# Picking and returning the experts' tokens by TensorE in a mixture-of-experts layer, and v by token in the dilated attention

## The reference, cut to what matters

```python
def expert_block(args):                      # 32 experts, two for each token
    tok_b, e = args
    xb = xpad[tok_b]                         # 64 slots: rows of the normalised tokens
    h = jax.nn.silu(xb @ w_gate[e]) * (xb @ w_up[e])     # 1024 -> 2 x 512
    return h @ w_down[e]                     # 512 -> 1024
out = out.reshape(rows, d) * buf_wt[:, None]
y = jnp.zeros((t + 1, d)).at[buf_tok].add(out)[:t]       # weighted, added back by token
...
q, k, v, z = jnp.split(h @ w_in, [G * E, 2 * G * E, 2 * G * E + E], axis=-1)   # dilated_mixer
```

## Time and profile before

| | us |
|---|---|
| median of 3 runs | 1627.55 (1623.54 to 1627.7) |
| the profiled execution | 1623.5 |
| its span, first to last instruction | 1621.7 |
| PE busy | 1405.4 (87% of the span) |
| DVE busy | 658.9 (41%) |
| ACT busy | 482.8 (30%) |
| POOL busy | 84.6 (5%) |

### The profile page before, as it was taken

One profiled execution on the slowest core, in us unless ns is written; L12 is line 12 of the kernel. 1 busy time (PEld: TensorE's weight loads), 2 busy tenths in 40 slices (PEclk: granted clock), 3 DMA queues, 4 the chain that ended last, 5 costly groups with the idle time before them and its releaser, 6 DMA issues.

```text
span 1621.7 us, 17185 instructions
## 1 busy us (share of the span) xinstructions
PE 1405.4 (87%) x6530; PEld 946.7 (58%) x6530; DVE 658.9 (41%) x1144; ACT 482.8 (30%) x717; POOL 84.6 (5%) x139
## 2 busy tenths in 40 slices
PE   6999996997787779878739999989999999999976
PEld 5787774332222323322227888767788878878765
DVE  4567746010000000000065656545555654565545
ACT  6462431110000000100153222334444534544432
POOL 2010001110000000100021010000000000000000
PEclk9999996999889999988959999989999999999988
DMA  8737338999999999999774553221212122121001
GB/s 356 306 130 271 145 113 322 348 386 393 399 406 400 385 385 404 373 395 395 318 287 144 207 195 130 104 80 52 104 52 104 53 78 79 61 96 52 1 1 65
DMA packets 41004, 347.71 MB, mean 214 GB/s; under 512 B 6080, under 2 KB 6208, under 8 KB 22592
## 3 DMA queue, kind: packets, MB, share of 16 engines
q1 hardware_dynamic: 29632, 304.69, 48.3%
q0 software_dynamic: 10304, 38.84, 7.0%
q10 hardware_dynamic: 960, 2.70, 0.4%
HBM read 321.56 MB, written 24.64 MB: 213 GB/s over the span
## 4 chain that ended last, share of the span: by engine, by line
PE 48%; DVE 3%; ACT 2%; issue 2%; DMA 1%; DVEq 0%; POOL 0%; SPq 0%; ACTq 0%; POOLq 0%
PE ps L259 46%; PE ps L649 1%; ACT ar L798 1%; DVE b_NL L1242 0%; DVE ar L1234 0%; DMA ar<-y_scratch,rt 0%; PE ps L708 0%; DVE hres L1676 0%; ACT ar L811 0%; PE ps L265 0%; DVE hres L1669 0%; ACT b_NH L807 0%; DMA y_scratch<-ar 0%; DVE ar L1856 0%; ACT ar L1012 0%
## 5 line engine op out<-in xcount | busy, mean ns | idle before, releaser
L259 PE MATMUL ps<-ring,ar 128*64 128x512 f32 x720 | 266.8, 640 | 61.5 <-issue 49.2
L259 PE MATMUL ps<-ar 128*128 128x128 f32 (+6 forms) x1022 | 290.5, 439 | 12.8 <-DVE ar L1587 4.6
L259 PE MATMUL ps<-b_NH,b_WH 128*128 128x512 f32 x768 | 203.7, 401 | 9.3 <-ACT b_NH L807 4.2
L1617 DVE TENSOR_TENSOR ar<-ar,ps 128x256 f32<-128x256 f32 x34 | 14.3, 422 | 482.1 <-ACT ar L939 482.1
L259 PEld LDWEIGHTS ps<-ring,ar 128*64 128x64 f32 x720 | 78.3, 146 | 224.0 <-issue 206.2
L259 PE MATMUL ps<-b_NH,b_WL 128*128 128x512 f32 x768 | 197.4, 393 | 0.0
L259 PE MATMUL ps<-b_NL,b_WH 128*128 128x512 f32 x768 | 190.4, 391 | 0.0
L1175 DVE TENSOR_TENSOR b_WL<-ring,b_WH 128x1024 fp32r<-128x1024 f32 x112 | 136.7, 1221 | 99.5 <-ACT b_WH L750 99.5
L259 PEld LDWEIGHTS ps<-b_NH,b_WH 128*128 128x128 f32 x768 | 142.1, 190 | 40.7 <-ACT b_NH L807 8.9
L259 PEld LDWEIGHTS ps<-b_NH,b_WL 128*128 128x128 f32 x768 | 145.9, 190 | 30.6
L259 PEld LDWEIGHTS ps<-b_NL,b_WH 128*128 128x128 f32 x768 | 144.9, 189 | 30.2
(11 more groups left out here) (260 smaller groups left out, 1550.7 us busy)
## 6 DMA issues: line engine op xcount, KB each, us to landing
ring<-in_wts_dram SPq DMA_DIRECT2D x79, 2048.0 KB, 17.4
spare<-in_wts_dram SPq DMA_DIRECT2D x31, 2048.0 KB, 37.4
ar<-in_wts_dram SPq DMA_DIRECT2D x22, 2048.0 KB, 39.7
ring<-in_wmod_dram SPq DMA_DIRECT2D x24, 512.0 KB, 5.0
ar<-in_wmod_dram POOLq DMA_DIRECT2D x24, 512.0 KB, 4.2
y_scratch<-gate POOLq DMA_DIRECT2D x11, 1024.0 KB, 21.1
y_scratch<-ar SPq DMA_DIRECT2D x68, 128.0 KB, 31.7
hres<-in_x_dram SPq DMA_DIRECT2D x4, 512.0 KB, 5.9
```

The lines of the kernel that those rows point to most:

```text
L259: return pe.matmul(o, l, m, start=start, stop=stop, skip_group_check=True)
L1617: return dve.tensor_tensor(hh[s], sg[s], ps[:, b, 256:512], ALU.mult)
```

## The change

The rows of an expert are picked by a product with a matrix of ones and noughts, and its results are brought to their tokens by a product with a matrix of weights and noughts and added to `hres` by DVE from PSUM. The gathers, stores, both DRAM copies, the noughts and the table are gone. The experts' buffers are single (two for `ysb`); the panels have eight slots. Each expert's result is returned during the next expert, a second block's within its own turn.

```diff
+            def rows_in(b):
+                for p in range(4):
+                    mm(ps[0:64, b, :], OH[:, p, :], xs[:, p, 0:512], p == 0, p == 3)
+                    t = mm(ps[64:128, b, :], OH[:, p, :], xs[:, p, 512:1024], p == 0, p == 3)
+            def turn_x(b):
+                for j in range(4):
+                    t = pe.transpose(ps[:, b, j * 128:(j + 1) * 128], xg[:, j * 128:(j + 1) * 128], ident[:, :])
-            def turn_x(s, b):
-                for k in range(8):
-                    t = pe.transpose(ps[:, b, k * 64:(k + 1) * 64], xg[s][0:64, k * 128:(k + 1) * 128],
-                                     ident[0:64, 0:64])
+            def rows_out(ys, p, b, sem):
+                for hf in range(2):
+                    r = slice(64 * hf, 64 * hf + 64)
+                    mm(ps[:, b + hf, :], OT[r, p * 128:(p + 1) * 128], ys[r, :], True, True).then_inc(S[sem], 1)
+            def main_out(n, p):
+                if p == 0:
+                    pe.wait_ge(S["m_ot"], n + 1)
+                    pe.wait_ge(S["m_y"], n + 1)
+                if 8 * n + 2 * p >= 2:
+                    pe.wait_ge(S["m_ad"], 8 * n + 2 * p)
+                rows_out(ysb[n % 2], p, 6, "m_sc")
```

PE's order in one expert after the change (waits on panels and buffers left out), and for a second block:

```diff
             for n in range(NE):
+                up(xT, 0, (panel(i), panel(i + 1))).then_inc(S["m_up"], 1)
+                if n:
+                    main_out(n - 1, 0)
                 pe.wait_ge(S["m_hh"], n + 1)
+                turn_h(4).then_inc(S["m_d1"], 1)
+                    rows_in(2).then_inc(S["m_gx"], 1)
+                if n:
+                    main_out(n - 1, 1)
+                down(5, panel(i + 2)).then_inc(S["m_d2"], 1)
+                    turn_x(3).then_inc(S["m_tx"], 1)
+                if n:
+                    main_out(n - 1, 2)
+                    main_out(n - 1, 3)
                 with pe.If(second(n)):
+                    rows_in(2).then_inc(S["o_gx"], 1)
+                    turn_x(3).then_inc(S["o_tx"], 1)
+                    up(xT2, 1, (panel(i), panel(i + 1))).then_inc(S["o_up"], 1)
+                    turn_h(4).then_inc(S["o_d1"], 1)
+                    down(5, panel(i + 2)).then_inc(S["o_d2"], 1)
+                    for p in range(4):
+                        if p:
+                            pe.wait_ge(S["o_ad"], 8 * n + 2 * p)
+                        rows_out(ysb[1 - n % 2], p, 6, "o_sc")
+                    pe.wait_ge(S["o_ad"], 8 * n + 8)
```

```diff
+            def pick_in(n, sem, e, ne):
+                dve.tensor_scalar(rel, sl_f, float(-CAP * n), None, ALU.add).then_inc(S[e], 1)
+                dve.tensor_tensor(eq, bc(mid(i_n[:, 0:CAP]), 128, 8, CAP), bc(last(rel), 128, 8, CAP),
+                                  ALU.is_equal).then_inc(S[e], 1)
+                dve.tensor_tensor(OH, eq[:, 0:4, :], eq[:, 4:8, :], ALU.add).then_inc(S[sem], 1)
+            def pick_out(n, sem, e, ne):
+                for c, o in enumerate((OT, ot1)):
+                    dve.scalar_tensor_tensor(out=o, in0=slrow[c], scalar=jn[:, n:n + 1], in1=wrow[c], op0=ALU.is_equal,
+                                             op1=ALU.mult).then_inc(S[e], 1)
+                dve.tensor_tensor(OT, OT, ot1, ALU.add).then_inc(S[sem], 1)
+            def add_out(p, hf):
+                h = hres[:, p, hf * 512:hf * 512 + 512]
+                return dve.tensor_tensor(h, ps[:, 6 + hf, :], h, ALU.add)
```

In the dilated attention v is projected by token in two panels after head 0's first four tiles (`token_panel(P_V, ...)`, 96 products each, as many as eight v tiles had), and ACT evicts it straight to `vall`. The other 56 tiles follow through three banks in place of two, and the last two are the z tiles of heads 6 and 7, behind which attention steps 0 and 1 of head 7 lie:

```diff
-                    if j == 3:
-                        pe.wait_ge(S["vc"], h + 1)
-                        for q in range(4):
-                            t = pe.transpose(ps[:, 5, q * 128:(q + 1) * 128], sw[(7 * h + 6) % 2][:, q * 128:(q + 1) * 128],
-                                             ident[:, :])
-            for step in range(6):
+            for step in range(2, 6):
                 attention(7, step)
```

More of the change, by code:

```diff
@@ L713, in tensor_program, with first, behind @@
-            for step in range(6):
+                h, r = TILES[g]
+                if r == 6:
+                    pe.wait_ge(S["z"], h + 1)
+                else:
+                    pe.wait_ge(S["ra"], 6 * h + r + 1)
+            def first(j):
+                if j == 3:
+                    proj_free(0)
+            def behind(g):
+                if g >= 7:
+                    proj_free(g - 3)
+            b4 = tuple(PROJ[g % 3] for g in range(4))
+            lead_panel(P_DIL, op_b, N_DL, b4)
@@ new lines, in tensor_program @@
+            run(feature_tiles(P_DIL, op_b, b4, (2, 3), first))
+            token_panel(P_V, op_b, (2, 3, 4, 6))
+            proj_free(3)
+            pe.wait_ge(S["vk"], 2)
+            token_panel(P_V + 1, op_b, (7, 0, 2, 3))
+            proj_free(1)
+            proj_free(2)
+            for q in range(1, 14):
+                i = P_V + 1 + q
+                b4 = tuple(PROJ[(4 * q + j) % 3] for j in range(4))
+                for j in feature_tiles(i, op_b, b4, range(4), lambda j, q=q: behind(4 * q + j)):
+                    h, step = step_behind(4 * q + j)
+                    if h >= 0 and step < 6:
+                        attention(h, step)
@@ L935, in scalar_program, with copy_x @@
             act.activation(ex, t1_, ACT.Exp).then_inc(S["rt_act"], 1)
[L938 to L945 removed]
+            def copy_x():
+                return act.activation(xg, ps[:, 2, :], ACT.Copy)
@@ new lines, in silu_gate, with copy_h, copy_y, copy_rows @@
+            def silu_gate(b):
+                return act.activation(sg, ps[:, b, 0:256], ACT.Silu)
+            def copy_h():
+                return act.activation(hT.rearrange("p a b -> p (a b)"), ps[:, 4, 0:256], ACT.Copy)
+            def copy_y(s):
+                return act.activation(ysb[s], ps[:, 5, :], ACT.Copy)
+            def copy_rows(dst, u):
+                act.wait_ge(S["rw"], u + 1)
+                for c in range(2):
+                    act.activation(dst[c], ps[:, 6 + c, :], ACT.Copy).then_inc(S["rwc"], 1)
@@ L1151, in scalar_program @@
-            for step in range(6):
+            for g in range(4):
+                if g < 2:
+                    hi(P_DIL, g + 2)
+                elif g == 3:
+                    hi(P_V, 0)
+                rope(g)
+            for c in range(2):
+                for n in range(4):
+                    next_hi(P_V + c, n)
+                for t in range(4):
+                    evict(P_V + c, t, vall[:, t, c * 512:(c + 1) * 512], ACT.Copy, "vk",
+                          ((2, 3, 4, 6), (7, 0, 2, 3))[c][t])
@@ L1152, in scalar_program @@
+            for g in range(4, 56):
+                next_hi(tile_panel(g), g % 4)
+                if TILES[g][1] < 6:
+                    rope(g)
+                else:
+                    silu_z(g)
+                h, step = step_behind(g)
+                if h >= 0 and step < 6:
+                    attention(h, step)
+            for step in range(2, 6):
                 attention(7, step)
-            act.wait_ge(S["wdone"], done(cno(P_DIL + 15, 3)))
+            act.wait_ge(S["wdone"], done(cno(P_DO - 1, 3)))
```

718 lines of the change are left out of this document (327 added, 391 removed).

## The result

| | before | after |
|---|---|---|
| median, us | 1626.01 (4 runs, 1623.54 to 1627.70) | 1875.89 (4 runs, 1870.31 to 1880.77) |
| span of the profiled execution | 1621.7 | 1876.5 |
| PE busy | 1405.4 (87%) | 1670.4 (89%) |
| DVE busy | 658.9 (41%) | 936.3 (50%) |

What follows compares the result with a forecast made beforehand. The prediction took DMA bytes to bound the experts and TensorE the dilated attention, with TensorE bounding the experts after. It summed 1623.5 + 192 (experts) - 1 (start) - 3.5 (tail) - 15 (v) = 1796 us, range 1735 to 1860.

Steps and rivals of the forecast that it cites:

- pure column time: Experts: TensorE's products alone, before any wait, take 17.9 us per expert, above the 16.2 us at which DMA would bind.
- The turn: Experts 1 to 30: products, returns, waits and branch in order on TensorE sum to 20.8 us per expert.
- about 0.4 shows: Each expert: of PE's branch on second(n), about 0.4 us is not covered by queued products, estimated from ACT's dozen branches.
- Rival 2: Experts: idle bursts halve PE's clock, costing 1.7 us per turn, +54 us in all, 1850 us; chance 0.07.
- The second blocks: Two experts' extra blocks become a chain of products, waits and returns on PE: 32 us each, 64 us together.
- Twelve branches (1.9 us on DVE): Tail after the last expert: returns, these branches and pick_out bring the first addition to about +10 us; tail -3.5 us.
- The start: From slot numbers to the first up: picking replaces gathering, first up at about 276 us, -1 us, at best -5.
- v by token: Dilated attention: ACT-eviction waits and four transposes per head go, and head 7's steps move earlier: -15 us.
- The changes between kinds of product: Experts on TensorE: 0.1 us at each switch of product kind, about nine per expert; uncertainty 0 to 0.2 us each.
- Serial halves (1): Returns: products on the two row halves take turns, +2.6 us per expert, +81 in all, 1881 us; chance 0.08.
- DMA stays the bound (3): Experts: PE has room, so the stage shrinks to its panels' 479 us, -51, total 1553 us; chance 0.03.
- A hidden wait (4): Experts: PE's queue hides the fourth return's wait, branches cost nothing: 18.8 us per expert, 1728 us; chance 0.07.

Runs made afterwards that it cites:

- experiment 3: The changed kernel with each expert's fourth return in two other PSUM banks, so it no longer waits for the third's additions: 1784.22 us, ratio 1.099.
- experiment 4: The changed kernel without any branch among the experts, second and overflow blocks left out, the fourth return's wait kept: 1739.03 us in one execution.
- experiment 1: The twelve untaken overflow-block branches removed on all engines: from the changed kernel 1844.39 us, ratio 1.136; from the kernel before 1621.64 us, ratio 0.998.
- experiment 8: The kernel before with only the changed dilated attention: 1611.47 us, ratio 0.991; with the twelve overflow branches also inside one: 1609.19 us.
- experiment 5: The kernel of experiment 3 with each product of the returns issued twice into the same bank: 1891.30 us in one execution.

## Why the prediction was right or wrong

**The bound and the sign: right.** TensorE became the bound and DMA fell to 0.63. The forecast's 17.9 us of pure column time, above the panels' 16.3 (16.2 in the forecast), decided it; experiment 3, whose plain turns have no wait left, puts 19.2 us on TensorE.

**The turn, 20.8 us forecast, 21.6 measured.** The single term most in error is the branch, "about 0.4 shows": it costs 0.76 (experiment 4). The wait was 1.37, not 1.6, and the products with their changes together some 0.65 more than the 18.8: the fourth return takes 1.13 in place of 0.9, and no other part is off by more than 0.15. Over 30 turns that is +24 us. Taking ACT's dozen branches as the price of PE's was the weak choice: ACT's are 0.15 us apart, while PE's branch and what stands around it hold its queue for 1.8 us, of which the fourth return covers 1.1.

**The clock: wrong to leave out as small.** Rival 2 had 0.07 and 1.7 us per lost turn. The price was right (1.65), the number of turns was neither all nor none but 7 of 28: +12 us. The forecast treated the clock as a case of its own, and so its sum held nothing for it.

**The second blocks, 32 us forecast, 38 measured:** +12. The chain was right; the forecast ran it at 2.4 GHz, although its rival 2 says that PE stands idle for half of their returns.

**The tail, the largest error.** "Twelve branches (1.9 us on DVE)" is the step that failed: -3.5 forecast, +27.1 measured. The 1.9 us are ACT's, from the earlier trace rows (DVE's own twelve take 2.1 in that trace), and the walk of PE itself, 28.6 us in the kernel after, was left out of the sum. The kernel before has it in its trace (15.9 us), inside the 25.25 us that its timeline puts down to ACT before the first transposes:

```profile
832.68 1.94 PE L265 MATMUL ps<-ident,ar 128*128 128x128 f32 x8 [25.25 <-ACT ar L1016]
```

This is a step that was moved past a queue: the last returns now stand behind branches that nobody waited for before. Experiment 1 shows it: without the branches the tail is 25.5 us shorter. The +-5 for start and tail were drawn without this row, and without this error the time would have lain inside the range, near its upper end.

**The start, -1 forecast:** from slot numbers to the first silu it is 22.4 to 22.7 us in the five profiles of the old form and 16.3 to 16.6 in the eight of the new, 6 us less. Half of this lies before the first up (12.5 us before, 9.3 after), which is what the forecast's -1 to -5 was about, and half in that up itself (10.3 and 7.1 us): rows_in now runs ahead of it, and the granted clock is back at 2.4 GHz when it starts. In this execution slot numbers came 6.2 us late, as TensorE ran at half clock from 153 to 167 us in code that the change does not touch; three of the five profiles of the old form have such a stretch there too.

**v by token, -15 forecast:** -14.8, and -13.6 to -14.9 alone (experiment 8).

**The changes between kinds of product.** The sum had 0.1 us at each, from one row; the two forms of return (1.06 us alone, 0.86 and 0.2 in experiment 5) give the same. The Trainium skill (TensorEngine Tiling, Key Properties) says that a change of tiling mode drains TensorE; the trace agrees in that a return's second pair and the product behind it each start some 0.1 us behind the steady pace. A turn has eight changes (the forecast says about nine), some 0.8 us of 21.6.

**The rivals.** Serial halves (1): refuted by the records' starts, 0.007 us apart, and by experiment 5. DMA stays the bound (3): refuted by DMA at 0.63 and by experiment 3. A hidden wait (4): experiment 3 builds that kernel, and it takes 19.2 us per turn where 18.8 were forecast. Of the 80 us missed in all, 24 are the turn, 12 the clock, 12 the second blocks, 30 the tail; what is left is under the spread of the runs.

## What to carry to other kernels

Moving work from a queue that is the bound to an engine with slack pays only as far as the slack goes: 4 us of TensorE's time per expert were free, 9 were asked. When a step is moved, walk through every instruction that will now stand ahead of it on its engine, skipped branches too, and look for their time in the trace of before even where nobody waited for it. A wait on the critical engine costs more than its length: it empties the queue, lays bare the branch behind it, and may cost the clock; two spare banks gave back 92 us where the wait itself was 1.4 us a turn.

## What the runs showed of the hardware that was not expected

- An `If` block that is not entered can cost TensorE 2.7 to 5.1 us: eight of twelve did, each with one instruction packet of 16 KB starting within it, and the other four (0.2 to 0.3 us) had none; in the kernel before it was four of twelve. Over the ten profiles that have these blocks, 54 of the 55 that took 2.1 us or more have exactly one such packet, and 42 of the 43 others none. ACT and DVE passed their twelve, over much shorter bodies, in 1.9 and 2.4 us. One branch around all twelve cost TensorE 3.55 us. That the packets are code being fetched because of the jump fits all of this, but was not shown by itself.
- The granted clock fell to 1.2 GHz in 16 plain turns of the three kernels with 1.37 and 0.76 us of idle close together, in none of the 30 turns with 1.37 alone, and in none without either. Which turns it hits differs from kernel to kernel.
- Products of 64 rows on the two row halves run at the same time: their records start 0.007 us apart, and 16 records with 512 columns take 3.63 us, the changes of kind included.
- Added products can cost nothing where TensorE else stands idle: with the returns doubled, the two second blocks did not get longer: over them the granted clock was 1.2 GHz for 3.4 us in place of 34.
